# Four columns of room behind each slot of a weight ring, in a one-core trunk layer

## The chip, the core and the metric

The kernel runs on one NeuronCore of a Trainium2 chip, in one launch. The metric is the device time in microseconds (us) of that core. Everything in the text that is not said otherwise is float32 or float32r, the 4-byte type in which TensorE takes its operands here.

## What is computed

One inference step of a decoder layer over 2048 prompt tokens and 8 sequences of 4 sample tokens. Each sub-layer normalises its input by its root mean square (RMSNorm), multiplies it with a weight matrix, and adds the normalised result to the residual x. Cut to the products, which are what TensorE spends its time on, it is:

```python
h = rmsnorm(x, g_mix_pre);  z = h @ w_in                # 1024 -> 3072 (+ 8 gate columns)
a = silu(group_layernorm(causal_dwconv(z_value * sigmoid(z_gate)), groups=4))   # width 31
hm = mlstm_chunkwise(q, k, v, i, f)                     # 4 heads of 128
x = x + rmsnorm(concat(a, hm) @ w_out)                  # 1024 -> 1024
up = causal_dwconv(rmsnorm(x) @ w_up)                   # 1024 -> 5632, width 3
x = x + rmsnorm((gelu(up[:, :2816]) * up[:, 2816:]) @ w_down)     # 2816 -> 1024
x = x + (p @ w_ple) * sigmoid(rmsnorm(x) @ w_ple_gate)  # 256 -> 1024 and 1024 -> 1024
```

All of it is float32, and the output has to agree with it closely enough that a product of rounded operands alone does not do. So each product is made of three: every operand is split into a high part (rounded to float32r) and a low part (the rest), and high x high, high x low and low x high are added up in PSUM.

## The kernel before

The 2080 tokens are five blocks of 416 (`NBLK`, `T`). Features lie on the 128 partitions and tokens along the free axis, so a matmul takes 128 x 128 weights as its stationary operand and 128 x 416 activations as its moving one. The five blocks run one after the other through the whole layer (`program(blk, last, mid)` of each engine), and TensorE's instructions are written out for all of them.

**The weight ring.** The weights are cut into 108 units a block. A unit is eight blocks of 128 columns, split into a high part and a low part: 2 x 1024 columns of 4 bytes, 8192 bytes on each partition. The tensor `w_split` (called `w`) has three slots of one unit (`RING`); unit u lies in slot u % 3. `split_product` (L671 to L675) takes one block out of a slot: L673 multiplies the high weights with the high activations, L674 the high weights with the low activations, L675 the low weights with the high activations. So one unit is 8 x 3 = 24 matmuls, each with its own weight load.

**How a slot is filled.** In the first block (the opening) a unit comes from the input in two halves of 512 columns into `w_raw`; ScalarE rounds each half into the slot (`high_part`, L1067), GpSimd or VectorE subtracts to get the low part (`low_part`, L657 or L2337), and SyncE's queue stores the whole slot into the DRAM tensor `w_kept` (`keep`, L542). In the blocks after it SyncE loads slots from `w_kept` (`load_split`, L560, and `load_next`, L600). Both move one run of 8192 bytes for each of the 128 partitions, 1024 KB in all. A load for unit u waits until TensorE has used unit u - 3, and TensorE waits before a unit's first block until the slot is filled. What runs when is set by the order in which the instructions are written and by semaphores; there is no scheduler.

**Where things lie.** SBUF tensors are laid one behind the other along a partition, each start rounded up to 32 bytes. `f_room` and `f_split` start at byte 16512, `h_split` at 53120, `w_split` at 79744, which is 1246 x 64. A slot is 8192 bytes, a part 4096 and a block 512, all multiples of 64, so every weight block starts at a multiple of 64 bytes. The text calls a start address modulo 64 its residue. Other tensors have other residues: the gate weights `wg_split` are blocks of 36 columns, 144 bytes, so that they start at residues 0, 16, 32 and 48 in turn; the keys `k_tok`, inside `out_room` behind 5 x 129 columns, start at residue 20; the exponentials `wexp` in `temp_room` start at 16 and 48 in turn and the queries in `qkv` at 0 and 32; the sample tokens' window `a_dec` starts at residue 32 and has runs of 120 bytes, 136 bytes apart.

Of the kernel before, what the change touches and what calls it, by code (L numbers as in the profile page):

```python
# [10 lines left out]
F32R = mybir.dt.float32r  # L11
# [3 lines left out]
P = 128  # L15
D = 1024
KD = D // P
# [33 lines left out]
RING = 3  # L51
# [220 lines left out]
def hymba_layer(nc, t):  # L272
    ctx = ExitStack()
    with ctx:
        def sb(name, shape, dt=F32):
            return ctx.enter_context(nc.sbuf_tensor(name, shape, dt))
# [7 lines left out]
            pass  # L284
        f_room = sb("f_room", [P, FH * 2 * T])
        h = sb("h_split", [P, KD, 2, T], F32R)
        w = sb("w_split", [P, RING, 2, KD * P], F32R)
        wg = sb("wg_split", [P, 2, KD, GATES], F32R)
        with nc.sbuf_tensor("w_spare", [P, 2, KD * P], F32R) as w_spare:
            pass  # L290
# [2264 lines left out]
```

## Time and profile before

| | us |
|---|---|
| median of 3 runs | 2705.51 |
| lowest, highest run | 2704.6, 2708.81 |
| profiled execution, first to last instruction | 2707.0 |
| TensorE (PE) busy in it | 2676.2 (99%) |
| weight loads (PEld) busy | 2589.0 (96%) |
| VectorE (DVE) busy | 1729.9 (64%) |
| ScalarE (ACT) busy | 921.2 (34%) |
| GpSimd (POOL) busy | 237.0 (9%) |

The page gives for the profiled execution its span alone. It lies 1.5 us over the median of the runs and inside their spread. Rows of the trace name an instruction by its line, its engine, its operation, and its tiles as output<-moving,stationary. PE and PEld are two rows of one engine: the weight load of the next matmul lies beside the matmul that runs. A matmul's record covers its way through the array, so that two follow each other more closely than one is long; the step from one start to the next is the measure. The granted TensorE clock was 0.96 or more of the full 2.4 GHz in every stretch of the span.

### The profile page before, as it was taken

How to read it: one execution, taken by the hardware profiler on the slowest of the kernel's cores; microseconds unless marked ns; L12 is line 12 of the kernel's file. 1: busy time of each engine (PE TensorE's matmuls, PEld its weight loads, DVE VectorE, ACT ScalarE, POOL GpSimd, SP SyncE). 2: the span in 40 equal slices, each digit the busy share in tenths (PEclk: the TensorE clock that was granted, in tenths of full speed). 3: DMA queues.
4: the chain of work that ended last, by engine and by line, in shares of the span. 5: the costliest groups of instructions: out<-in, count | busy, mean ns of one | idle time of the engine just before them, and what ended most of it. 6: DMA issues, size and time to landing. Idle time of an engine off the chain costs nothing.

```text
span 2707.0 us, 37694 instructions
## 1 busy us (share of the span) xinstructions
PE 2676.2 (99%) x14549; PEld 2589.0 (96%) x14549; DVE 1729.9 (64%) x3699; ACT 921.2 (34%) x1932; POOL 237.0 (9%) x180
## 2 busy tenths in 40 slices
PE   9999999999999999999999999999999999999999
PEld 7989999999999999999999999999999998899998
DVE  8975898865566665555665664756866636472645
ACT  5464434453432122443321233532112425211113
POOL 4432515230000000000000000000000000000000
PEclk9999999999999999999999999999999999999999
DMA  9857989877566666565666666566666676466665
GB/s 329 318 192 272 361 333 364 324 276 297 187 230 231 231 233 232 206 253 202 230 228 235 231 226 254 193 220 227 229 233 231 213 285 145 171 240 231 233 232 203
DMA packets 125117, 660.59 MB, mean 244 GB/s; under 512 B 22010, under 2 KB 22654, under 8 KB 55182
## 3 DMA queue, kind: packets, MB, share of 16 engines
q1 hardware_dynamic: 111150, 628.29, 64.3%
q10 hardware_dynamic: 13792, 29.92, 3.4%
q8 instruction: 116, 1.90, 0.3%
q14 instruction: 59, 0.48, 0.1%
HBM read 533.04 MB, written 125.11 MB: 243 GB/s over the span
## 4 chain that ended last, share of the span: by engine, by line
PE 92%; DVE 4%; ACT 2%; DMA 1%; issue 1%; POOL 0%; SPq 0%; DVEq 0%; ACTq 0%; POOLq 0%
PE proj L673 29%; PE proj L674 28%; PE proj L675 28%; PE m L673 1%; PE m L674 1%; PE m L675 1%; DMA w_split<-w_kept 1%; PE m L857 1%; PE m L890 1%; PE m L891 0%; PE m L851 0%; PE m L868 0%; DMA w_raw<-in_w_units 0%; PE m L719 0%; DVE cv L1848 0%
## 5 line engine op out<-in xcount | busy, mean ns | idle before, releaser
L673 PE MATMUL proj<-h_split,w_split 128*128 128x416 f32 x2704 | 969.7, 359 | 4.1 <-DVE h_split L1782 1.9
L674 PE MATMUL proj<-h_split,w_split 128*128 128x416 f32 x2704 | 947.2, 350 | 0.0
L675 PE MATMUL proj<-h_split,w_split 128*128 128x416 f32 x2704 | 942.1, 348 | 0.0
L673 PE MATMUL proj<-f_split,w_split 128*128 128x416 f32 x1536 | 549.9, 358 | 10.3 <-POOL w_split L657 3.1
L674 PE MATMUL proj<-f_split,w_split 128*128 128x416 f32 x1536 | 539.2, 351 | 0.0
L675 PE MATMUL proj<-f_split,w_split 128*128 128x416 f32 x1536 | 536.1, 349 | 0.0
L673 PEld LDWEIGHTS proj<-h_split,w_split 128*128 128x128 f32 x2704 | 507.3, 188 | 15.3 <-issue 5.7
L675 PEld LDWEIGHTS proj<-h_split,w_split 128*128 128x128 f32 x2704 | 508.2, 188 | 9.9
L674 PEld LDWEIGHTS proj<-h_split,w_split 128*128 128x128 f32 x2704 | 508.6, 188 | 3.5 <-issue 1.4
L673 PEld LDWEIGHTS proj<-f_split,w_split 128*128 128x128 f32 x1536 | 288.9, 188 | 26.1 <-issue 6.1
L1825 DVE SCALAR_TENSOR_TENSOR cv<-a_ext,vecs,cv 128x416 f32<-128x416 f32 (+1 forms) x480 | 304.9, 684 | 0.0
L675 PEld LDWEIGHTS proj<-f_split,w_split 128*128 128x128 f32 x1536 | 289.5, 188 | 5.7
L674 PEld LDWEIGHTS proj<-f_split,w_split 128*128 128x128 f32 x1536 | 289.6, 189 | 1.3
L1487 ACT ACTIVATE temp_room<-proj 128x416 f32<-128x416 f32 x176 | 91.5, 520 | 560.2 <-PE proj L675 560.0
L657 POOL TENSOR_TENSOR w_split<-w_raw,w_split 128x512 fp32r<-128x512 f32 x176 | 236.8, 1367 | 379.5 <-ACT w_split L1067 379.5
L2296 DVE SCALAR_TENSOR_TENSOR m<-temp_room,vecs,m 128x416 f32<-128x416 f32 (+1 forms) x440 | 257.0, 653 | 0.0
L2326 DVE TENSOR_TENSOR f_split<-m,f_split 128x416 fp32r<-128x416 f32 x110 | 65.1, 592 | 238.6 <-ACT f_split L1499 238.6
L2293 DVE TENSOR_SCALAR m<-temp_room,vecs 128x416 f32<-128x416 f32 (+1 forms) x220 | 146.0, 710 | 65.3 <-ACT temp_room L1487 65.2
L1701 DVE TENSOR_TENSOR mix_room<-mix_room,temp_room 128x416 f32<-128x416 f32 x131 | 80.8, 617 | 105.9 <-ACT temp_room L1085 100.3
L1067 ACT ACTIVATE w_split<-w_raw 128x512 fp32r<-128x512 f32 x216 | 124.5, 624 | 11.8 <-DMA w_raw<-in_w_units 11.4
L1495 ACT ACTIVATE mix_room<-m 128x416 f32<-128x416 f32 (+1 forms) x110 | 57.4, 522 | 128.9 <-DVE m L2296 128.8
L2379 DVE TENSOR_TENSOR out_room<-out_room,temp_room 128x416 f32<-128x416 f32 x40 | 23.5, 591 | 100.2 <-ACT temp_room L1530 100.2
(308 smaller groups left out, 2285.5 us busy)
## 6 DMA issues: line engine op xcount, KB each, us to landing
w_split<-w_kept SPq DMA_DIRECT2D x430, 1024.0 KB, 4.8
w_kept<-w_split SPq DMA_DIRECT2D x108, 1024.0 KB, 6.6
w_raw<-in_w_units SPq DMA_DIRECT2D x216, 256.0 KB, 4.8
x_resid<-in_x ACTq DMA_DIRECT2D x5, 1664.0 KB, 12.5
out_y<-x_resid ACTq DMA_DIRECT2D x8, 832.0 KB, 7.7
rows<-in_x ACTq DMA_DIRECT2D x4, 832.0 KB, 7.0
w_raw<-in_x ACTq DMA_DIRECT2D x3, 832.0 KB, 8.7
qkv<-in_p ACTq DMA_DIRECT2D x5, 416.0 KB, 5.3
```

The lines of the kernel that those rows point to most:

```text
L657: nc.gpsimd.tensor_tensor(w[:, slot, 1, cols], w_raw[:, r % RAW, cols], w[:, slot, 0, cols].bitcast(F32), ALU.subtract).then_inc(s_w[slot] ...
L673: mm(dst, w_hi, a_hi, start=first, stop=False)
L674: mm(dst, w_hi, a_lo, start=False, stop=False)
L675: return mm(dst, w_lo, a_hi, start=False, stop=last)
L1067: fn(w[:, u % RING, 0, cols], w_raw[:, r % RAW, cols], ACT.Copy).then_inc(s_hi.sem, 1)
L1487: fn(s[:, n, 2:2 + T], src, ACT.Copy).then_inc(s_evac.sem, 1)
L1495: fn(gelu_out[:, j % 3, 0:wide], facc_of(j, last)[0][:, 0:wide], ACT.Gelu_apprx_tanh).then_inc(s_fgelu.sem, 1)
L1701: v.tensor_tensor(sq_sum, none if i == 1 else sq_sum, tile, ALU.add).then_inc(s_squse.sem, 2 if i == 1 else 1)
L1825: ins = v.scalar_tensor_tensor(acc[:, 0:n], a_ext[:, c, k:k + n], wt, acc[:, 0:n], ALU.mult, ALU.add)
L2293: ins = v.tensor_scalar(dst, src, wt, col("b_conv_ffn", n * FT + j), ALU.mult, ALU.add)
L2296: ins = v.scalar_tensor_tensor(dst, src, wt, dst, ALU.mult, ALU.add)
L2326: v.tensor_tensor(f[:, j % FH, 1, :], facc_of(j, last)[1][:, 0:T], f[:, j % FH, 0, :].bitcast(F32), ALU.subtract).then_inc(s_f.sem, 1)
```

## The change

The ring's tensor gets four columns of 4 bytes behind each slot, and `w` becomes a view of it without them.

```diff
         h = sb("h_split", [P, KD, 2, T], F32R)
-        w = sb("w_split", [P, RING, 2, KD * P], F32R)
+        w_slots = sb("w_split", [P, RING, 2 * KD * P + 4], F32R)
+        w = w_slots[:, :, 0:2 * KD * P].rearrange("p r (s e) -> p r s e", s=2)
         wg = sb("wg_split", [P, 2, KD, GATES], F32R)
```

Slots are now 8208 bytes apart. In the built program `w_split` still starts at 79744, so that the blocks of slot 0 stay at residue 0, those of slot 1 start at residue 16 and those of slot 2 at residue 32. The tensor grows by 48 bytes, and with the rounding of starts every tensor behind it (from `wg_split` on) moves up by 64 bytes and keeps its residue. The activations `f_split` and `h_split` do not move. Every engine has the same instructions in the same order, with the same shapes and the same waits; one line more in the file moves all line numbers behind it by one. A slot's 8192 bytes on a partition are still one run, for a DMA as for an engine, and the four columns are neither written nor read.

## Rows read from the trace of the kernel before

**Rows 1.** Page, head and part 1: span, and busy time by engine.
```profile
span 2707.0 us, 37694 instructions
PE 2676.2 (99%) x14549; PEld 2589.0 (96%) x14549; DVE 1729.9 (64%) x3699; ACT 921.2 (34%) x1932; POOL 237.0 (9%) x180
```

**Rows 2.** Page, part 4: the chain that ended last, by line.
```profile
PE proj L673 29%; PE proj L674 28%; PE proj L675 28%; PE m L673 1%; PE m L674 1%; PE m L675 1%; DMA w_split<-w_kept 1%; PE m L857 1%; PE m L890 1%; PE m L891 0%; PE m L851 0%; PE m L868 0%; DMA w_raw<-in_w_units 0%; PE m L719 0%; DVE cv L1848 0%
```

**Rows 3.** Line L673: weight loads, ns min/median/max; then PE's idle time by releaser.
```profile
L673 PEld LDWEIGHTS proj<-h_split,w_split x2704: 186/187/334, 20.3 to 2662.0; 128*128 128x128 f32 x194
L673 PEld LDWEIGHTS proj<-f_split,w_split x1536: 186/187/337, 156.4 to 2701.2; 128*128 128x128 f32 x192
L673 PEld LDWEIGHTS m<-h_split,wg_split x40: 110/112/115, 56.8 to 2151.8; 128*36 128x36 f32 x40
L673 PEld LDWEIGHTS m<-f_split,w_split x40: 186/187/188, 166.7 to 2692.1; 128*128 128x128 f32 x40
L673 PEld LDWEIGHTS m<-h_split,w_split x24: 187/187/334, 2351.6 to 2377.8; 128*128 128x128 f32 x24
...
  DMA w_split<-w_kept: 3.1, 3
  POOL w_split L657: 3.1, 1
```

**Rows 4.** Timeline of PE, 57 to 64.5 us: start, us, instruction.
```profile
56.99 0.35 PE L673 MATMUL m<-h_split,wg_split 128*36 128x416 f32 x1
...
61.52 0.35 PE L673 MATMUL proj<-h_split,w_split 128*128 128x416 f32 x1
...
64.35 0.35 PE L673 MATMUL proj<-h_split,w_split 128*128 128x416 f32 x1
```

**Rows 5.** Lines L868, L891 and L890: weight loads of other tensors, ns min/median/max.
```profile
L868 PEld LDWEIGHTS m<-mix_room,out_room x120: 186/190/193, 99.7 to 2292.8; 104*128 104x128 f32 x96, 96*128 96x128 f32 x24
L891 PEld LDWEIGHTS m<-mix_room,qkv x160: 161/168/173, 106.0 to 2297.3; 128*104 128x104 f32 x128, 128*96 128x96 f32 x32
L890 PEld LDWEIGHTS m<-out_room,temp_room x160: 159/168/172, 105.7 to 2297.0; 104*104 104x104 f32 x128, 96*96 96x96 f32 x32
```

**Rows 6.** Timeline of PE, 168.8 to 171.2 us: eight bf16 matmuls.
```profile
169.09 1.58 PE L706 MATMUL m<-mask_b,sel_b 128*128 128x416 bf16 x8
```

**Rows 7.** Windows: us, busy us by engine, granted clock, DMA share, GB/s.
```profile
core 0: us, PE busy (x) PEld busy (x) DVE busy (x) ACT busy (x) POOL busy (x), PEclk, DMA share, GB/s
270.00:405.00 135.00, 134.95 (x715) 133.20 (x714) 119.48 (x188) 56.18 (x119) 48.55 (x38) 1.00 0.93 347
405.00:540.00 135.00, 134.95 (x715) 133.23 (x714) 114.68 (x177) 62.17 (x132) 56.61 (x44) 1.00 0.93 347
632.00:1157.00 525.00, 524.31 (x2863) 511.29 (x2862) 317.63 (x666) 163.72 (x335) 0.00 (x0) 1.00 0.63 227
```

**Rows 8.** DMA, 270 to 540 us: queue, packets, MB, share of 16 engines; issues.
```profile
q1 hardware_dynamic: 25576, 93.41, 92.6%
...
w_kept<-w_split SPq DMA_DIRECT2D x59, 1024.0 KB, 6.6
w_raw<-in_w_units SPq DMA_DIRECT2D x116, 256.0 KB, 4.8
```

**Rows 9.** DMA, 632 to 2210 us.
```profile
q1 hardware_dynamic: 46717, 340.26, 60.1%
...
w_split<-w_kept SPq DMA_DIRECT2D x325, 1024.0 KB, 4.8
```

**Rows 10.** Line L560, the loads into the ring: who waited; issue to landing.
```profile
  PE proj L673: 3.1, 3
...
DMA to landing us min/median/max: 4.6/4.8/12.2
```

**Rows 11.** DMA, 22.9 to 31.2 us: ScalarE's queue, and the load of a_dec.
```profile
q10 hardware_dynamic: 4256, 0.85, 64.0%
...
a_dec<-in_a_dec ACTq DMA_DIRECT2D x1, 480.0 KB, 7.7
```

**Rows 12.** Tile w_split: the engines that write it, ns min/median/max.
```profile
L1067 ACT ACTIVATE w_split<-w_raw x216: 612/623/656, 10.9 to 613.6; 128x512 fp32r<-128x512 f32 x108
L657 POOL TENSOR_TENSOR w_split<-w_raw,w_split x176: 1268/1300/3257, 15.1 to 615.1; 128x512 fp32r<-128x512 f32 x176
```

## The prediction

> **What bounds the kernel now.** I read the busy times first. The span is 2707.0 us and TensorE's matmuls cover 2676.2 us of it [rows 1], so 31 us are left in which it does nothing. The chain of waits then says which matmuls these are: the three lines of the split product hold 29, 28 and 28% of the span [rows 2]. The rest of the case is therefore the step at which these matmuls follow each other, and whether the ring that feeds them is ever late.
>
> The rows of L673 count them. They read the ring 2704 + 1536 + 40 + 24 = 4304 times, and L674 and L675 as often: 12,912 matmuls [rows 3]. Their step comes from two starts, 61.52 and 64.35 us, with 15 steps between them: 2.83 / 15 = 188.7 ns [rows 4]. 12,912 x 188.7 ns = 2436 us, nine tenths of the span. The weight load beside each takes 187 ns at the median [rows 3], so the load path too is almost full: in the stretch from 632 to 1157 us it is busy 511.29 of 525 us [rows 7].
>
> The ring is almost never late: TensorE stood before L673 for 3.1 us on a load from DRAM and for 3.1 us on GpSimd's part, in the whole span [rows 3]. A ring that is filled faster can give back no more than these 6.2 us.
>
> **The change part by part.** It adds and removes no instruction and no wait. What differs is the start address of the blocks in slots 1 and 2, residues 16 and 32 in place of 0, for everyone who touches them: two thirds of 12,912, 8608 weight loads; the DMAs between these slots and DRAM; and the splits in the opening.
>
> Weight loads. The trace has no 128-column float32r load off residue 0, so I bound it. The nearest rows are the gate products: the same three lines, the same moving tensor, weight blocks at residues 0, 16, 32 and 48 in turn. Their 24 matmuls begin at 56.99 us and the next one at 61.52 us: 4.53 / 24 = 188.75 ns [rows 4], the step of the ring's own. All 40 loads of their L673 lie between 110 and 115 ns [rows 3]. They load 36 columns, not 128, so they say that the step does not mind the residue, and also that a shorter load does not shorten the step; they do not test a long load. For that there is L868, 128 columns at residue 20: 186/190/193 against 186/187 in the ring, with the same shortest and a median 3 ns longer [rows 5]. L891 at residues 0 and 32 and L890 at 16 and 48 have the same median, 168 ns [rows 5], so I read the 3 ns as that of short bursts of another kind of matmul and not as the residue's. The step leaves some 188.7 - 187 = 1.7 ns for a longer load. Upper end: 3 ns more, 1.3 of it past the room, 8608 x 1.3 = 11 us; if none of the room can be used, 8608 x 3 = 26 us. Lower end: the eight bf16 matmuls of 416 columns take 1.58 us, and without the 0.34 us of the last they step by 177 ns [rows 6]; if the float32r step were long because equal residues clash, 8608 x (188.7 - 177) = 101 us would go. I take zero, by the gate products, which are nearest in kind.
>
> DMAs. Between 632 and 2210 us, queue 1 moves 340.26 MB in 60.1% of 16 engines' 1578 us: 15,174 us of engine time, so 8192 bytes take 365 ns [rows 9]. A load has 8 such packets for each engine. A slot is free when its unit has been used, and is needed again two units later: 2 x 24 x 188.7 ns = 9.06 us. The median landing is 4.8 us [rows 10], so 4.2 us are spare, more than the 8 x 365 ns = 2.9 us by which a doubling would lengthen it. In these stretches a slower packet costs nothing: DMA share 0.63, with a third of the loads doubled 0.83.
>
> The opening is tighter: a DMA share of 0.93 while PE is busy for 134.95 of each 135 us [rows 7]. From 270 to 540 us, 59 slots are stored, 59 x 128 = 7552 packets of 8192 bytes, 2517 from each slot [rows 8]. The other 7% of 270 us x 16 engines is idle, 302 us of engine time. So slot 1's packets could each take 302 / 2517 = 120 ns longer, or those of slots 1 and 2 each 60 ns, before DMA sets the pace. By bytes, a packet there takes 8192 x (0.926 x 270 x 16 us) / 93.41 MB = 351 ns [rows 8]; the margin is a third of a packet, or a sixth. The nearest row off a multiple of 32 is the load of the sample window, 120-byte runs 136 bytes apart. Its queue moved 4256 packets in 64% of 8.3 us x 16, which is 20 ns each with the waiting for other queues in it [rows 11]. A fixed cost for a start off the grid is then under 20 ns a packet, 5035 x 20 = 101 us of engine time, which fits into the idle 302: nothing. A rate that falls over the whole packet is not excluded by so short a run. Were slot 1's packets twice as long, 2517 x 351 ns = 883 us of engine time would come on, 581 us past the idle 302, and over 16 engines that is 36 us. Lower end: even DMAs that cost nothing return only the 3.1 us above. I take zero.
>
> Splits. ScalarE writes a half in 623 ns and GpSimd in 1300 ns [rows 12]: 2 x (0.62 + 1.30) = 3.8 us after a slot is free, against 9.06 us. GpSimd's 2.6 us for a unit could grow by 1.7 times before it fills the 24 x 188.7 ns = 4.53 us that TensorE takes. So both ends are zero, unless a write became that much slower, for which no row speaks.
>
> The sum is 2707.0 + 0 for the profiled execution, which lies 1.5 us over the median of the runs; for the median it is 2705.5 + 0 = **2705.5 us**. What a measurement of this kernel can tell from no change is 0.2%, 5.4 us.
>
> **The rivals.**
> *Longer weight loads (slower).* In slots 1 and 2 a load crosses one more boundary and takes 2 to 3 ns longer. PEld is full [rows 7], so past 1.7 ns it sets the step. Price 8608 x 1.3 to 3 ns, +11 to +26 us: 2717 to 2731. For it: the 190 ns of L868. Against: L890 as short as L891, and the gate products [rows 4, 5].
> *The opening becomes DMA-bound (slower).* Packets from slot 1, the one start that is not a multiple of 32, take half as long again or twice as long. It decides from 120 ns on. Half as long again: 2517 x 176 ns = 443 us, 141 past the idle 302, over 16 engines 9 us: 2714. Twice: 2742 by the 36 us above. For it: 0.93. Against: a_dec's 20 ns a packet, which includes its waits [rows 11].
> By the Trainium skill, "Collectives: The Full Stack", section "Rules for kernel authors", buffers should be aligned to 32 bytes, which "Prevents HW read-modify-write". The page says it of collectives; if it held for slot 1, the time would be this rival's 2714 to 2742. The 20 ns do not look like it.
> *A clash goes away (faster).* Weight reads disturb the moving reads, or a DMA's writes, as long as all starts agree modulo 64. A tenth of the 101 us would be 10 us: 2695; all of it 2604. For it: 188.7 against 177 ns. Against: the gate products mix all residues and keep the step [rows 4].
> That the change does not do what it says I leave out: the built addresses are 16 and 32 past a multiple of 64.
>
> **How the numbers follow.** No change 0.78, longer weight loads 0.08, DMA-bound opening 0.06, a clash that goes 0.08. Slower is 0.14, faster 0.08. No change lies within 5.4 us, 2700 to 2711. The range leaves out the far half of each rival: 2699 to 2722.
>
> **What would show it.** If I am right, the loads of L673 (now L674) keep 186/187 as their shortest and median, the step after 61.5 us stays 188.7 ns, the DMA share of 270 to 540 us stays 0.93 at the same 92 to 93% of queue 1, and PE is busy for all but 0.1 us of each 135 us there. Longer loads would show as a median of 189 or more, in two of three slots, with the span stretched in all five blocks alike. A DMA-bound opening would show as a share of 0.97 or more from 270 to 540 us, waits of SyncE's store or ScalarE's rounding on DMAs, and a last split by GpSimd that begins well after 615.1 us [rows 12], while the blocks after the opening keep their length. A clash that goes would show as a shorter step in the units of slots 1 and 2 alone. I am wrong if the time leaves 2700 to 2711 us.

## The result: slower by half a percent

The changed kernel takes 2720.37 us (median of 3 runs, 2718.6 to 2722.61) against 2705.51 us. The ratio is 1.0048, with a 95% interval of 1.0035 to 1.0062: 14.9 us slower where no change was forecast. The profiled execution takes 2718.6 us from first to last instruction.

### The profile after

Head and part 1 of the page of the changed kernel, the answer to [rows 1]:

```profile
span 2718.6 us, 37694 instructions
PE 2688.0 (99%) x14549; PEld 2593.0 (95%) x14549; DVE 1730.2 (64%) x3699; ACT 919.1 (34%) x1932; POOL 236.9 (9%) x180
```

The span grew by 11.6 us and PE's busy time by 11.8 us. TensorE still stands idle for 30.6 us, against 30.8 us before. So no new wait shows: the same matmuls follow each other more slowly.

The windows of the changed kernel, with the columns of [rows 7], say the same by counts:

```profile
270.00:405.00 135.00, 134.96 (x711) 132.73 (x710) 120.16 (x190) 55.60 (x118) 47.97 (x38) 1.00 0.92 344
405.00:540.00 135.00, 134.96 (x712) 132.72 (x711) 114.19 (x176) 61.52 (x132) 56.66 (x44) 1.00 0.93 343
```

In 135 us in which PE never rests there are 711 and 712 matmuls where there were 715. The granted clock is 1.00 in both, and the DMA share has not risen. The DMA view of 270 to 540 us and that of the ring's loads (now line L561) show queues and landings as they were [rows 8, 10]:

```profile
q1 hardware_dynamic: 25382, 92.63, 92.1%
...
w_kept<-w_split SPq DMA_DIRECT2D x58, 1024.0 KB, 6.5
```

```profile
  PE proj L674: 4.5, 3
...
DMA to landing us min/median/max: 4.6/4.8/11.9
```

Three loads were late, as before, for 4.5 us together instead of 3.1. The weight loads have the shortest and the median of [rows 3]:

```profile
L674 PEld LDWEIGHTS proj<-h_split,w_split x2704: 186/187/330, 19.9 to 2673.5; 128*128 128x128 f32 x194
```

So by every row that the prediction wanted to look at first, except the step, it looks right. The step that it named, the 15 after the gate products, is 189.4 ns now (2841 ns from the start at 61.35 us); it was 188.4 (2826 ns, which the rounded starts of [rows 4] show as 188.7). What happened to the ring's step shows in the timeline of PE. These are the starts of four units in slots 0, 1, 2 and 0, each 24 matmuls after the one above it, in a stretch without a pause. First the kernel before (start, us, instruction):

```profile
800.27 0.35 PE L673 MATMUL proj<-h_split,w_split 128*128 128x416 f32 x1
...
804.81 0.35 PE L673 MATMUL proj<-h_split,w_split 128*128 128x416 f32 x1
...
809.34 0.35 PE L673 MATMUL proj<-h_split,w_split 128*128 128x416 f32 x1
...
813.88 0.35 PE L673 MATMUL proj<-h_split,w_split 128*128 128x416 f32 x1
```

And the changed kernel, the same units:

```profile
804.08 0.35 PE L674 MATMUL proj<-h_split,w_split 128*128 128x416 f32 x1
...
808.62 0.35 PE L674 MATMUL proj<-h_split,w_split 128*128 128x416 f32 x1
...
813.20 0.35 PE L674 MATMUL proj<-h_split,w_split 128*128 128x416 f32 x1
...
817.75 0.35 PE L674 MATMUL proj<-h_split,w_split 128*128 128x416 f32 x1
```

Before, a unit takes 4.53 us in each slot and three take 13.60. After, it takes 4.54 us in slot 0, 4.58 in slot 1 and 4.55 in slot 2, and three take 13.67. In the trace's nanoseconds, which the timeline rounds, the units are 4533 before and 4538, 4583 and 4552 after, and the 59 gapless stretches of three units that read `h_split` have 13,600 and 13,673 ns as their medians. The 4304 blocks are 538 units, 179.3 for each slot, so 179.3 x 73 ns = 13.1 us. The two profiles differ by 11.6 us and the medians by 14.9, so this accounts for the loss within the scatter of the runs. The units in slots 1 and 2, whose weights start 16 or 32 bytes past a multiple of 64, step more slowly, in all five token blocks alike.

### The profile page after: what moved, and what is told of

The parts are those of the page before. It is cut to its first block, busy times and chain, and to the rows that moved or that the text cites. A ratio compares the mean times of both kernels' runs of the same rounds, so it can differ in the third digit from the quotient of the medians.

```text
span 2718.6 us, 37694 instructions
## 1 busy us (share of the span) xinstructions
PE 2688.0 (99%) x14549; PEld 2593.0 (95%) x14549; DVE 1730.2 (64%) x3699; ACT 919.1 (34%) x1932; POOL 236.9 (9%) x180
## 4 chain that ended last, share of the span: by engine, by line
PE 93%; DVE 4%; ACT 2%; DMA 1%; issue 0%; POOL 0%; SPq 0%; DVEq 0%; ACTq 0%; POOLq 0%
PE proj L674 29%; PE proj L676 28%; PE proj L675 28%; DMA w_split<-w_kept 1%; PE m L674 1%; PE m L675 1%; PE m L858 1%; PE m L676 1%; PE m L891 1%; PE m L852 1%; PE m L892 1%; PE m L869 0%; PE m L720 0%; DVE small L1946 0%; PE m L911 0%
## 5 line engine op out<-in xcount | busy, mean ns | idle before, releaser
L676 PE MATMUL proj<-h_split,w_split 128*128 128x416 f32 x2704 | 950.3, 351 | 0.0
L675 PE MATMUL proj<-h_split,w_split 128*128 128x416 f32 x2704 | 949.2, 351 | 0.0
L675 PE MATMUL proj<-f_split,w_split 128*128 128x416 f32 x1536 | 540.9, 352 | 0.0
L676 PE MATMUL proj<-f_split,w_split 128*128 128x416 f32 x1536 | 540.9, 352 | 0.0
L676 PEld LDWEIGHTS proj<-h_split,w_split 128*128 128x128 f32 x2704 | 508.2, 188 | 9.4
L675 PEld LDWEIGHTS proj<-h_split,w_split 128*128 128x128 f32 x2704 | 508.5, 188 | 8.5 <-issue 1.4
L676 PEld LDWEIGHTS proj<-f_split,w_split 128*128 128x128 f32 x1536 | 289.7, 189 | 5.1
L675 PEld LDWEIGHTS proj<-f_split,w_split 128*128 128x128 f32 x1536 | 289.7, 189 | 3.8
```

What stands on the lines that cost most here:

```text
L675: mm(dst, w_hi, a_lo, start=False, stop=False)
L676: return mm(dst, w_lo, a_hi, start=False, stop=last)
```

## The experiments

Each moves start addresses or shortens one thing. The measure beside the time is the same three units near 800 us, in which `h_split` is read, and three near 730 us, in which `f_split` is. "One run" stands where there is no ratio. The runs `short`, `fix0` and `narrow` further below do not compute the layer and are read by their steps.

| kernel | weight residues | time, before on that chip, us | ratio (95%) | 3 units, h / f, us |
|---|---|---|---|---|
| before | 0, 0, 0 | 2705.51 | | 13.60 / 13.60 |
| after | 0, 16, 32 | 2720.37, 2705.51 | 1.0048 (1.0035 to 1.0062) | 13.67 / 13.67 |
| all16 | 16 | 2730.76, 2708.27 | 1.0085 (1.0068 to 1.0102) | 13.76 / 13.76 |
| all32 | 32 | 2718.78, 2708.27 | 1.0039 (1.0025 to 1.0053) | 13.65 / 13.65 |
| all48 | 48 | 2707.88, 2708.27 | 1.0002 (0.9992 to 1.0012) | 13.60 / 13.60 |
| pad64 | 0, room behind | 2707.28, 2708.27 | 0.9997 (0.9987 to 1.0006) | 13.60 / 13.60 |
| act16 | 0, moving 16 | 2722.2, 2708.25 | 1.0046 (1.003 to 1.0063) | 13.76 / 13.60 |
| both16 | 16, moving 16 | 2718.73, 2708.25 | 1.0037 (1.0025 to 1.005) | 13.68 / 13.60 |
| act48 | 0, moving 48 | 2707.89, 2708.25 | 0.9998 (0.9989 to 1.0008) | 13.60 / 13.60 |
| m16 | 32, 48, 0, moving 16 | 2706.12, 2708.09 | one run | 13.59 / 13.53 |
| m32 | 0, 16, 32, moving 32 | 2713.22, 2706.67 | one run | 13.61 / 13.65 |
| m48 | 16, 32, 48, moving 48 | 2713.6, 2706.67 | one run | 13.67 / 13.61 |
| fine_a | 4, 24, 44 | 2709.37, 2708.09 | one run | 13.64 / 13.64 |
| fine_b | 52, 56, 60 | 2726.69, 2708.09 | one run | 13.73 / 13.73 |
| placed | 0, moving 16 | 2701.95, 2708.29 | 0.9977 (0.9968 to 0.9986) | 13.60 / 13.60 |

### The residue of the ring alone: all16, all32, all48

The slots follow each other without room, and the whole ring is moved by 4, 8 or 12 columns, so that all three slots have one residue:

```diff
-        w = sb("w_split", [P, RING, 2, KD * P], F32R)
+        w_slots = sb("w_split", [P, RING * 2 * KD * P + 16], F32R)
+        w = w_slots[:, 4:4 + RING * 2 * KD * P].rearrange("p (r s e) -> p r s e", r=RING, s=2)
```

(8 or 12 in place of 4 in all32 and all48.)

> All three slots start at residue 16, 8192 bytes apart as before; the tensors behind the ring move up by 64 bytes as in the change. In the change a block of three matmuls (step from L673's start to the next block's) takes 572.3 ns in slot 1 (residue 16), 569.1 in slot 2 (residue 32) and 567.5 in slot 0, against 566.6 before. Theory A, the start of a weight block modulo 64 sets the step: 572 ns in all slots, 4304 blocks x 5.7 ns = +24 us over before. Theory B, what costs is that the slots differ from each other, TensorE reading at one residue while a DMA fills another: 566.6 ns, +0 us. Theory C, the moved tensors behind the ring, or their place modulo more than 64, cost: some +12 us, the same for every kernel of this set.

> All three slots at residue 32. Theory A: 569 ns a block, 4304 x 2.4 = +10 us. Theory B: +0 us. Theory C: +12 us.

> All three slots at residue 48, which neither kernel has. Theory A in the form that the count of 32-byte pieces that 512 bytes touch sets it (17 from 16 and from 48, 16 from 0 and from 32) with a smaller part for 64-byte pieces (9 from 16, 32, 48): 572 ns, +24 us. Theory A in the form that the distance from 64 counts: between 567 and 576 ns, other than residue 16. Theory B: +0 us.

Three units of all16, then of all32, in the timeline of PE:

```profile
803.66 0.35 PE L674 MATMUL proj<-h_split,w_split 128*128 128x416 f32 x1
...
817.42 0.35 PE L674 MATMUL proj<-h_split,w_split 128*128 128x416 f32 x1
```

```profile
803.21 0.35 PE L674 MATMUL proj<-h_split,w_split 128*128 128x416 f32 x1
...
816.86 0.35 PE L674 MATMUL proj<-h_split,w_split 128*128 128x416 f32 x1
```

13.76 and 13.65 us: every slot now does what slots 1 and 2 did in the changed kernel (3 x 4.58 and 3 x 4.55). Residue 16 for all costs 22.5 us and residue 32 for all 10.5 us, so the mean of 0, 22.5 and 10.5 is 11 us; the 14.9 of the change has an interval of 9.5 to 16.8. Theory B falls, since the slots of all16 agree with each other and cost most. Residue 48 costs nothing, which fells the form of theory A that counts the pieces of 32 and 64 bytes that a row of weights touches: from 48 the 512 bytes touch as many as from 16, 17 and 9.

By the Trainium skill, "SBUF — State Buffer", section "Specifications (TRN2)", SBUF works in lines of 16 bytes and a crossing into a new line has a price. All four residues are starts of such lines, so by that rule all four kernels would be alike; all16 is not.

### The tensors behind the ring: pad64

Sixteen columns of room behind each slot. The slots stay at residue 0, and the room and the move of everything behind the ring remain. Against the kernel before:

```diff
-        w = sb("w_split", [P, RING, 2, KD * P], F32R)
+        w_slots = sb("w_split", [P, RING * 2 * KD * P + 48], F32R)
+        w_slots = w_slots[:, 0:0 + RING * (2 * KD * P + 16)].rearrange("p (r e) -> p r e", r=RING)
+        w = w_slots[:, :, 0:2 * KD * P].rearrange("p r (s e) -> p r s e", s=2)
```

> Sixteen columns (64 bytes) of room behind each slot: all slots at residue 0, but 8256 bytes apart, so that they differ modulo 128, and the tensors behind the ring move by 192 bytes. Theory A: 566.6 ns, +0 us. Theory B in the form that any difference between the slots costs: +12 us. Theory C: +12 us or so.

No change, with 13.60 us for three units. Neither the room nor the moved tensors cost anything, and theory C falls. The single units are not quite those of the kernel before: 4538, 4529 and 4532 ns in slots 0, 1 and 2, of which slot 1 lies 64 bytes off the others modulo 128. They add up to the same 13.60.

### The other operand: act16, act48, both16

The activations are moved by 4 or 12 columns and the ring stays at residue 0; in both16 the ring moves by 4 columns as well.

```diff
-        with nc.sbuf_tensor("f_split", [P, FH, 2, T], F32R) as f:
+        with nc.sbuf_tensor("f_split", [P, FH * 2 * T + 16], F32R) as f_all:
...
+        f = f_all[:, 4:4 + FH * 2 * T].rearrange("p (k s t) -> p k s t", k=FH, s=2)
...
+        h_room = sb("h_split", [P, KD * 2 * T + 16], F32R)
+        h = h_room[:, 4:4 + KD * 2 * T].rearrange("p (k s t) -> p k s t", k=KD, s=2)
```

> The ring as before at residue 0; the activations, f_split and h_split, start at residue 16 (f_room moves with f_split; whatever stands behind moves by multiples of 64 bytes). The runs so far: weights at 0, 16, 32, 48 give 566.7, 572.8, 569.3 and 566.7 ns a block. Theory W, the weights' own start sets the step: 566.7 ns, +0 us. Theory R, the weights' start counted from the moving operand's, modulo 64, sets it: 0 - 16 is 48, 566.7 ns, +0 us. Theory M, the moving operand's own start costs as the weights' does: 572 ns, +24 us.

> Weights at residue 0, activations at residue 48. Theory W: 566.7 ns, +0 us. Theory R: 0 - 48 is 16, 572.8 ns, +24 us. Theory M: between 566 and 573 ns, as the moving operand's own table has it.

> Weights and activations both at residue 16. Theory W: as with the weights alone at 16, 572.8 ns, +24 us. Theory R: the difference is 0 again, 566.7 ns, +0 us. Theory M: 572 ns or more, +24 to +48 us.

In act16 the products that read `h_split` and those that read `f_split` part (timeline of PE, two stretches of three units):

```profile
733.97 0.35 PE L676 MATMUL proj<-f_split,w_split 128*128 128x416 f32 x1
...
747.57 0.35 PE L676 MATMUL proj<-f_split,w_split 128*128 128x416 f32 x1
...
804.58 0.35 PE L676 MATMUL proj<-h_split,w_split 128*128 128x416 f32 x1
...
818.34 0.35 PE L676 MATMUL proj<-h_split,w_split 128*128 128x416 f32 x1
```

13.60 us for f and 13.76 for h, at one residue of both. So the moving operand's start counts too, and W and R, which said no change, are wrong here. That it counts like the weights' (M) is half wrong, since f keeps its step. The two do differ past the residue: `f_split` starts at 16528, and `h_split`, which the room ahead of it moves by 64 bytes more, at 53200. Modulo 128 that is 16 and 80; no run separates the two moves. That only the difference of the two residues counts (R) fails on both16, which at difference 0 is slower than before by 0.37%, and on act48, which is not slower.

### How long a weight load holds TensorE: short

The changed kernel, with the middle of the three products (L675 here) cut to 128 of its 416 columns; the rest of that product is left out. A load longer than this matmul can no longer hide.

```diff
-                mm(dst, w_hi, a_lo, start=False, stop=False)
+                mm(dst[:, 0:128], w_hi, a_lo[:, 0:128], start=False, stop=False)
```

> The changed kernel (slots at 0, 16 and 32) with one of the three products, high weights x low activations (L674 of before), cut to the first 128 of 416 columns; the rest of that product is left out, so the time is far shorter and says nothing. Read by slot: the step from this matmul to the next, beside which the low weights are loaded. Theory L, a weight load takes longer at residues 16 and 32 and is what the step waits for: with a short moving operand the step is the load's, near 187 ns or what a load really takes, and longer by 2 to 6 ns in slot 1 and 1 to 3 in slot 2. Theory S, the load and the moving reads get in each other's way and the moving stream is slowed: the step behind the short matmul is the same in all slots to 1 ns, and the other two steps keep their differences.

Timeline of PE and of its loads (PEld) in slot 0:

```profile
800.14 0.35 PE L674 MATMUL proj<-h_split,w_split 128*128 128x416 f32 x1
800.14 0.19 PEld L675 LDWEIGHTS proj<-h_split,w_split 128*128 128x128 f32 x1
800.33 0.22 PE L675 MATMUL proj<-h_split,w_split 128*128 128x128 f32 x1
800.33 0.19 PEld L676 LDWEIGHTS proj<-h_split,w_split 128*128 128x128 f32 x1
800.39 0.40 PE L676 MATMUL proj<-h_split,w_split 128*128 128x416 f32 x1
800.44 0.19 PEld L674 LDWEIGHTS proj<-h_split,w_split 128*128 128x128 f32 x1
800.62 0.35 PE L674 MATMUL proj<-h_split,w_split 128*128 128x416 f32 x1
```

The load of L676 begins at 800.33 with a record of 0.19 us, yet the next load begins 0.11 us later. The matmul that needs the weights begins 0.06 us after its load, and its record of 0.40 us is 0.05 longer than that of the other matmuls of 416 columns: 0.11 us again. So a load's record is not the time for which the load path is taken. That is about 110 ns, the mean over all blocks, and the same to 1 ns in the slots at residues 0, 16 and 32. By the Trainium skill, "TensorE: Matmul & The Clock Gate", section "LDWEIGHTS (loading the stationary operand)", a load takes its columns divided by 1.2 ns, for 128 columns an estimate of 107 ns; the 110 ns agree with it, and the record of 187 ns does not. Loads of 110 ns lie wholly beside a matmul that steps at 189 ns, and they are not longer off residue 0. Theory L falls. Theory S is not borne out either: in blocks without a pause the step of the short matmul differs by more than 1 ns (57.8, 60.5 and 58.7 ns), and the whole block has lost most of its difference (487.6, 488.6 and 488.4 ns, against 567.5, 572.5 and 568.9 in the changed kernel). The run clears the loads; it does not show where in the moving stream the time goes.

### Reads or writes: fix0

The ring at residue 16, as in all16. From the second token block on TensorE takes all weights from one fixed place at residue 0 in `wg_split`, so its results there are not the layer's; everyone who writes the ring goes on as in all16.

```diff
+                        hi, lo = home[:, 0, cols], home[:, 1, cols]
+                        if blk:
+                            hi = lo = wg[:, 0, :, :].rearrange("p k e -> p (k e)")[:, 0:P]
...
```

> The ring at residue 16 in all slots, filled as ever; but from the second token block on, every product of the ring reads its weights from one fixed place at residue 0, the first 128 columns of the gate weights. What the products compute is left out with that. Theory E (TensorE's own weight reads carry the cost): a block takes 567 ns from the second token block on and 572.8 in the first, +5 us over before. Theory D (the writes into the ring, by DMA and in the opening by ScalarE and GpSimd, carry it): 572.8 ns throughout, +24 us.

Two stretches of three units, in the first token block and in the second:

```profile
273.41 0.35 PE L674 MATMUL proj<-h_split,w_split 128*128 128x416 f32 x1
...
287.17 0.35 PE L674 MATMUL proj<-h_split,w_split 128*128 128x416 f32 x1
...
803.61 0.35 PE L674 MATMUL proj<-h_split,wg_split 128*128 128x416 f32 x1
...
817.15 0.35 PE L674 MATMUL proj<-h_split,wg_split 128*128 128x416 f32 x1
```

13.76 us with the ring's weights at residue 16, 13.55 with the fixed ones (13,547 ns), while the DMAs still write at residue 16. The whole run takes 2707.11 us against 2706.67 on that chip, where D said 24 us more. So it is TensorE's own read of the weights that counts and not who writes them (E holds, though its 567 ns a block is 564.5, and D falls). And 13.55 is less than the 13.60 of the kernel before: that was not the floor. This lower step belongs to one place that is loaded again for every matmul, so it is no row for a ring.

### Short loads: narrow

The changed kernel, in which all blocks of a product but its first and last (six of eight in most products that read `h_split`) load 36 of 128 columns. The other 92 output rows of these blocks are left out.

```diff
+                if not first and not last:
+                    dst, w_hi, w_lo = dst[0:36], w_hi[:, 0:36], w_lo[:, 0:36]
```

> The changed kernel (slots at 0, 16, 32), in which every block of a product but its first and its last loads 36 weight columns in place of 128; the other 92 output rows of these blocks are left out. The moving operand keeps its 416 columns. Theory P, the weight reads and the moving reads that run beside them clash, and how often depends on both starts: the load is 36/128 as long, and the 4.7 ns between slot 1 and slot 0 shrink to some 1.3, the 1.5 of slot 2 to some 0.4. Theory Q, an operand off its line costs once, at its start: 4.7 and 1.5 ns stay.

The mean of these narrowed blocks, without those that hold a pause, is 569.4 ns in slot 0, 567.0 in slot 1 and 564.4 in slot 2; the same blocks of the changed kernel have 567.0, 572.7 and 568.9. The differences neither shrink nor stay: slot 0 becomes the slowest and slot 2 the fastest. Both forms fail, and blocks of 36 columns say nothing on blocks of 128.

### Looking for the rule: m16, m32, m48, fine_a, fine_b

Combinations of both shifts, and starts off the 16-byte grid. In m16, m32 and m48 the activations move by 4, 8 or 12 columns, and the ring has four columns of room behind each slot as in the changed kernel; fine_a starts the ring at column 1 with 5 columns of room, fine_b at column 13 with 1. The ring of fine_b, against the kernel before:

```diff
-        w = sb("w_split", [P, RING, 2, KD * P], F32R)
+        w_slots = sb("w_split", [P, RING * 2 * KD * P + 16], F32R)
+        w_slots = w_slots[:, 13:13 + RING * (2 * KD * P + 1)].rearrange("p (r e) -> p r e", r=RING)
+        w = w_slots[:, :, 0:2 * KD * P].rearrange("p r (s e) -> p r s e", s=2)
```

> Activations at residue 48, slots at 16, 32 and 48: three pairs of starts in one kernel, read by slot. So far in ns a block (weights, moving): (0,0) 566.7, (16,0) 572.8, (32,0) 569.3, (48,0) 566.7, (0,16) 570.5, (16,16) 569.1, (0,48) 566.8. Theory W+M, each start has its own cost and they add up, fails already at (16,16), which it puts at 576.6; here it says 572.8, 569.3, 566.7. Theory R, the difference alone, fails at (0,16), which it puts at 566.7; here it says 569.3, 566.7, 566.7. Theory P, both starts count together and neither sum nor difference does it: other values, none below 566 if 566.7 is the stream's own.

> Activations at residue 32, slots at 0, 16 and 32. Theory R: 569.3, 566.7, 566.7. Theory W+M: a common amount over 566.7, 572.8, 569.3. Theory P: other values, none below 566.

> Activations at residue 16, slots at 32, 48 and 0. Table so far, ns a block by weights' residue 0, 16, 32, 48: moving at 0: 566.7, 572.8, 569.3, 566.7; at 16: 570.5, 569.1; at 32: 569.7, 566.9, 566.1; at 48: 566.8, 569.7, 568.0, 568.9. Theory P1, both starts count in steps of 16 bytes, with no part for what lies behind them: slot 2 (residue 0) repeats 570.5; the other two between 566 and 573. If the step has more to it than the two starts (the order of the blocks, the rhythm that the loads fall into), slot 2 is off by over 1 ns.

> Activations at residue 0, slots at 4, 24 and 44, off the 16-byte grid. Theory G16, reads go in lines of 16 bytes: 4 to 12 bytes past a line cost a further line, so all three lie above the value of the line they start in: over 566.7, over 572.8 and over 569.3. Theory G0, the step goes smoothly from one tabled value to the next: some 568, 571 and 567.

> Activations at residue 0, slots at 52, 56 and 60. Theory G16: over 566.7, the value at 48, in all three alike. Theory G0: 566.7 in all three, as at 48 and at 64.

No table by residue modulo 64 survives. In m16 the slot with weights at 0 and activations at 16 takes 4489 ns a unit for f and 4537 for h, where act16, with the same two residues and the activations at the same addresses, has 4533 and 4587 (P1 said a repeat). Those 4489 ns, 561 a block, are also below the 566 that theory P gave as the floor for m32 and m48. In m32 the slots take 4550, 4535 and 4528 ns with h, as theory R said to a nanosecond a block, but in m48 (4580, 4536 and 4557 ns with h) R is some 3 ns a block off in slots 0 and 2, and W+M in slots 1 and 2. fine_b has its three slots inside the one line from 48 to 63, whose start costs nothing in all48, and is among the slowest (timeline of PE, three units):

```profile
801.49 0.35 PE L675 MATMUL proj<-h_split,w_split 128*128 128x416 f32 x1
...
815.21 0.35 PE L675 MATMUL proj<-h_split,w_split 128*128 128x416 f32 x1
```

13.73 us (13,727 ns), and 2726.69 us in all. fine_a, at 4, 24 and 44, is within 1.3 us of the kernel before on its chip; its units sum to 13.64 us, by which 179.3 x 40 ns = 7 us would be due, so the single time does not tell. Its slots 1 and 2 take 4535 and 4545 ns, 567 and 568 a block, under the 572.8 and 569.3 that G16 set as floors, and G0 is wrong on fine_b, for which it said 566.7. So 4 bytes matter, in a way that neither the line in which a row of weights starts nor the number of lines predicts.

### A better placing: placed

The best pair so far put at one place for both activations: weights at 64 modulo 512, f and h at 144 modulo 512, by 96, 4 and 52 columns of shift.

```diff
+        f = f_all[:, 4:4 + FH * 2 * T].rearrange("p (k s t) -> p k s t", k=FH, s=2)
...
+        h = h_room[:, 52:52 + KD * 2 * T].rearrange("p (k s t) -> p k s t", k=KD, s=2)
...
+        w = w_slots[:, 96:96 + RING * 2 * KD * P].rearrange("p (r s e) -> p r s e", r=RING, s=2)
```

> All weight blocks start at 64 modulo 128 (64 modulo 512) and all activations, f_split and h_split, at 16 modulo 128 (144 modulo 512): the pair that was shortest so far, 562.9 ns a block, in slot 2 of m16 with f_split as the moving operand, against 566.7 before. Theory P128, the two starts modulo 128 set the step: 563 ns a block with both operands, 4304 x 3.8 = -16 us against before, some 2692 us. If the step also hangs on what the neighbouring blocks do, or on the slots' distance: 565 to 568 ns, -7 to +6 us.

It beats both kernels: 0.9977 of the kernel before (0.9968 to 0.9986), 6 us, which is less than half of the expected 16, so P128 falls. The same instructions at the same addresses run at two steps in it, 13.60 us for three units near 2404 us and 13.44 near 1323 us:

```profile
1323.06 0.35 PE L677 MATMUL proj<-h_split,w_split 128*128 128x416 f32 x1
...
1336.50 0.35 PE L677 MATMUL proj<-h_split,w_split 128*128 128x416 f32 x1
...
2404.41 0.35 PE L677 MATMUL proj<-h_split,w_split 128*128 128x416 f32 x1
...
2418.01 0.35 PE L677 MATMUL proj<-h_split,w_split 128*128 128x416 f32 x1
```

### Addresses or the phase: placed2, act16b

Two kernels with two steps in one profile, each run once more unchanged.

> The kernel of the run placed once more, nothing changed, one look. In its first profile three gapless units took 13.60 us in most stretches, but 13.44 us in every stretch from 1249 to 1600 us (the third block of tokens), with the same instructions and the same start addresses as in the other blocks. Theory T (what surrounds a stretch, such as the DMA traffic or the instructions ahead of it, picks the rhythm): the same stretches, 1249 to 1600 us, are at 13.44 us again and the others at 13.60. Theory H (where TensorE stands after a pause, to some ns, picks one of several rhythms, which then holds until the next pause): the stretches at 13.44 us lie elsewhere this time, fewer or more of them; each stretch holds one rhythm from pause to pause. Theory A (the two start addresses alone set the step): 13.60 everywhere or 13.44 everywhere; the first profile already speaks against it.

> The kernel of the run act16 once more, nothing changed, one look. In its first profile the products that read h_split took 13.60 us for three gapless units in the first block's stretch from 259 to 362 us, and 13.76 us in the same stretch of the four blocks after it (from 791, 1320, 1849 and 2402 us). Theory T: 13.60 there and 13.76 in the four others again. Theory H: at least one of these five stretches is at another of the two values than before. Theory A: all five alike.

The same four places in placed2:

```profile
1324.76 0.35 PE L677 MATMUL proj<-h_split,w_split 128*128 128x416 f32 x1
...
1338.36 0.35 PE L677 MATMUL proj<-h_split,w_split 128*128 128x416 f32 x1
...
2410.61 0.35 PE L677 MATMUL proj<-h_split,w_split 128*128 128x416 f32 x1
...
2424.05 0.35 PE L677 MATMUL proj<-h_split,w_split 128*128 128x416 f32 x1
```

They have changed places: 13.60 us in the third block, 13.44 in the fifth. Of all gapless runs of eight blocks 19% had the short rhythm in placed (602 of 3188), 8% in placed2 (245 of 3191), and the spans are 2700.1 and 2705.7 us. At 53 ns a unit, 19% of 538 units are 5.4 us, nearly all that placed gains. The opening's stretch, first in act16 and then in act16b:

```profile
271.67 0.35 PE L676 MATMUL proj<-h_split,w_split 128*128 128x416 f32 x1
...
285.26 0.35 PE L676 MATMUL proj<-h_split,w_split 128*128 128x416 f32 x1
```

```profile
272.76 0.35 PE L676 MATMUL proj<-h_split,w_split 128*128 128x416 f32 x1
...
286.52 0.35 PE L676 MATMUL proj<-h_split,w_split 128*128 128x416 f32 x1
```

It was at 13.60 us (13.59 by the rounded starts) and is at 13.76. The fifth block's first stretch, from 2405 to 2464 us, went the other way, from 13.76 to 13.60. all16 has both 13.76 and, in one stretch, 13.44:

```profile
1789.04 0.35 PE L674 MATMUL proj<-f_split,w_split 128*128 128x416 f32 x1
...
1802.48 0.35 PE L674 MATMUL proj<-f_split,w_split 128*128 128x416 f32 x1
```

Theory A falls, and so does T in the form that the same stretches come out alike. Of H the runs bear out that one stretch takes another rhythm in another execution. That the place of TensorE after a pause picks it was argued and not tested; other things that differ between two executions, such as when DMAs land, are not excluded. "From pause to pause" fails: the third block of placed kept the short rhythm over several pauses, and at 1285.59 us it went from 567 to 560 ns a block with no step above 569 ns between.

## Why the prediction was wrong

**What bounds the kernel.** Right. PE's step set the time, and the whole loss is in it; a ring that is never late stayed so.

**Weight loads, the step that failed.** It was "I take zero, by the gate products, which are nearest in kind", with "the step after 61.5 us stays 188.7 ns" as its mark. The gate products were nearest in line and moving tensor, not in size: they load 36 columns where the ring loads 128. The prediction saw that they "do not test a long load" and chose their value all the same. In place of zero the runs show 2.1 ns a matmul in slot 1 and 0.8 in slot 2 (4583 and 4552 ns against 4533 for 24). By the ring's own steps a unit that visits residues 0, 16, 32 and 48 in turn would take (4533 + 4587 + 4552 + 4533) / 4 = 4551 ns; the gate's 24 matmuls take 4.53 us [rows 4]. That was one stretch of 24. The trace of the kernel before has a second in which the gate products are not interrupted, in its second token block:

```profile
569.80 0.35 PE L673 MATMUL m<-h_split,wg_split 128*36 128x416 f32 x1
...
574.35 0.35 PE L673 MATMUL proj<-f_split,w_split 128*128 128x416 f32 x1
```

It takes 4.55 us, 4545 ns against 4531 in the first, and in the changed kernel, where `wg_split` moved by 64 bytes and kept its residues, both take 4547. So the gate products do not keep one step, and a single stretch of them could not bear a zero. narrow shows from the other side that they are no stand-in for the ring: with 36-column loads the order of the slots turns round.

**The room of 1.7 ns.** Wrong in kind. It took a load's record of 187 ns for the time that the load path is taken; short shows 110 ns. So neither the room nor the 3 ns of L868 has to do with the loss.

**The rival of longer weight loads.** It named the place (slots 1 and 2, all blocks alike) and a price of 11 to 26 us that holds the 14.9, with a mechanism that the runs refute: the loads are as long as before. Its mark, a median of 189 ns or more, did not come. That its price fits is luck.

**The clash that goes.** It asked whether equal residues make the step long. Other starts do make it shorter at times, but by 0.16 us of 13.60 at most here, 1.2%, against the 101 us (6% of 8608 steps) that the bf16 step of 177 ns gave as its lower end. No gapless three units of any run that keeps the ring's products went below 13.44 us, 186.7 ns a step.

**DMAs, opening, splits.** Right, each at zero: landings of 4.8 and 6.5 us, a share of 0.92 to 0.93 from 270 to 540 us, PE idle for 0.04 us of 135.

What stays open is which pairs of start addresses allow which rhythms, and what in TensorE's reads makes them. The runs show that both operands' starts count, that 4 bytes count, that the residue alone does not settle it (m16 against act16, f against h in act16), and that the addresses alone do not either (placed2, act16b). That two operand streams meet at one memory is an idea that fits; no run here shows it.

## What to carry to other kernels

In a kernel that TensorE's 4-byte matmuls fill, the start addresses of both SBUF operands are a parameter worth about 1% (2702 to 2731 us here), and a harmless-looking pad cost half of that: try a few placings by their measured step, since no residue rule foretold it. Take the price of an unseen operand from a row of the same shape, or put both ends into the forecast. Of a record that lies beside another instruction, ask how soon the next one of its kind can start before you call the rest room.

## What was not expected of the hardware

- The step of the float32r matmul of 416 columns has several steady values, which repeat to a few nanoseconds over dozens of matmuls: three units (72 matmuls) take 13.44, 13.55, 13.60, 13.65, 13.67, 13.73 or 13.76 us, depending on the starts of the operands.
- One program at fixed addresses changes between two of them: 13.44 and 13.60 us in placed, 13.60 and 13.76 in act16, 13.44 and 13.76 in all16. In placed and act16 a second execution had them in other stretches.
- A load of 128 float32r columns shows a median record of 187 to 188 ns, and in short the next load starts 110 ns after it.
